# First stage of a hybrid decoder step: which engine scales the tokens and which makes their low part

## The reference, cut to what matters

```python
def rms_norm(x, g):
    xf = x.astype(jnp.float32)
    y = xf * lax.rsqrt(jnp.mean(xf * xf, axis=-1, keepdims=True) + EPS)
    return (y * g.astype(jnp.float32)).astype(x.dtype)

def hybrid_layer(x, attend, ...):
    n = rms_norm(x, g_mix)
    q, k, v, xr, gr, gates = jnp.split(n @ w_in, SPLITS, axis=-1)
    ...        # stick-breaking attention, RG-LRU branch, gates, w_out, ConvFFN, final norm
```

## Time and profile before

| | |
|---|---|
| median of 3 timed runs | 2435.93 us (2434.49 to 2438.55) |
| span of the profiled execution | 2431.0 us; the only time of that execution that is shown, 4.9 us under the median of the timed runs |
| PE busy in the span | 2178.0 us (90%) |
| DVE, ACT, POOL busy | 1433.5, 862.5, 331.6 us |
| first projection on PE starts | 51.31 us after the start of the span |

### The profile page before, as it was taken

How to read it: one execution, slowest core, us unless ns; L and a number is a source line. 1 busy time by engine, 2 the same in 40 slices (tenths; PEclk the granted TensorE clock), 3 DMA queues, 4 the chain that set the end, 5 groups by cost and what they waited for, 6 DMA issues and landing times. The chain is left out here.

```text
span 2431.0 us, 37753 instructions
## 1 busy us (share of the span) xinstructions
PE 2178.0 (90%) x12940; PEld 1926.8 (79%) x12940; DVE 1433.5 (59%) x2447; ACT 862.5 (35%) x1321; POOL 331.6 (14%) x151
## 2 busy tenths in 40 slices
PE   4997999999999999998999969789999999999986
PEld 3896777777777777777777747689999999999985
DVE  6002766767677676776768763364555554655645
ACT  4112454453544535445454452221222121222213
POOL 4122000000000000000001030031222211222210
PEclk9998998998989999999999979899999999999998
DMA  3333121031220302103021032211111111111104
GB/s 114 97 87 97 35 59 58 23 82 30 61 60 23 81 27 69 54 22 87 18 77 48 23 102 80 77 44 35 52 43 43 52 35 35 52 43 43 52 17 155
DMA packets 159829, 139.13 MB, mean 57 GB/s; under 512 B 19381, under 2 KB 147446, under 8 KB 159668
## 3 DMA queue, kind: packets, MB, share of 16 engines
q1 hardware_dynamic: 159694, 137.32, 19.1%
HBM read 119.86 MB, written 17.68 MB: 57 GB/s over the span
## 5 line engine op out<-in xcount | busy, mean ns | idle before, releaser
L87 PE MATMUL d_p_up<-n_hi,d_w_hi 128*128 128x350 f32 x1056 | 343.0, 325 | 14.0 <-POOL d_w_lo L1488 7.7
L87 PE MATMUL d_p_up<-n_hi,d_w_lo 128*128 128x350 f32 x1056 | 342.8, 325 | 0.0
L87 PE MATMUL d_p_up<-n_lo,d_w_hi 128*128 128x350 f32 x1056 | 342.5, 324 | 0.0
L1635 DVE TENSOR_TENSOR mix<-mix,d_p_down 128x350 f32<-128x350 f32 x264 | 137.3, 520 | 320.9 <-PE d_p_down L1682 320.9
L87 PE MATMUL b_p_proj<-n_hi,b_w_hi 128*128 128x350 f32 x768 | 294.8, 384 | 0.0
L1114 PE MATMUL b_p_av<-b_w_t,b_v_in 128*64 128x128 f32 (+2 forms) x1440 | 229.7, 291 | 36.1 <-DVE b_w_t L900 21.0
L87 PE MATMUL b_p_proj<-n_lo,b_w_hi 128*128 128x350 f32 x768 | 259.0, 337 | 0.0
L87 PE MATMUL b_p_proj<-n_hi,b_w_lo 128*128 128x350 f32 x768 | 258.9, 337 | 0.0
L1532 ACT ACTIVATE d_up<-d_p_up 128x350 f32<-128x350 f32 x132 | 60.8, 462 | 499.6 <-PE d_p_up L87 499.6
L797 POOL TENSOR_TENSOR b_w_lo<-w_raw,b_w_hi 128x1024 fp32r<-128x1024 f32 x33 | 84.2, 2553 | 1073.4 <-ACT b_w_hi L813 1073.4
L1114 PEld LDWEIGHTS b_p_av<-b_w_t,b_v_in 128*64 128x64 f32 (+1 forms) x1440 | 154.7, 140 | 94.1 <-issue 31.7
(11 more groups left out here) (241 smaller groups left out, 4429.5 us busy)
## 6 DMA issues: line engine op xcount, KB each, us to landing
w_raw<-in_w_in SPq DMA_DIRECT2D x45, 512.0 KB, 4.1
w_raw<-in_w_up SPq DMA_DIRECT2D x45, 512.0 KB, 3.9
b_page<-in_cache_k SPq DMA_DIRECT2D x128, 128.0 KB, 2.1
b_page<-in_cache_v SPq DMA_DIRECT2D x128, 128.0 KB, 2.0
w_raw<-in_w_down SPq DMA_DIRECT2D x22, 512.0 KB, 3.3
b_q_in<-q_scr SPq DMA_DIRECT2D x16, 264.1 KB
q_scr<-a_q_stage SPq DMA_DIRECT2D x16, 260.0 KB, 3.4
mix<-in_x_prompt SPq DMA_DIRECT2D x8, 512.0 KB, 7.0
```

The source lines that it names most:

```text
L87: last = pe.matmul(out, w[:, k, :], x[:, k, col:col + CW], start=(k == 0 and w is w_hi and x is x_hi), stop=(k == KT - 1 and w is w_lo))
L1635: dve.tensor_tensor(to, to, p_down[:, n % 4, 0:CW], ALU.add).then_inc(down_out, 1)
```

## The change

Two pieces of work move to another engine. The product of the tokens with their reciprocal root becomes an ACT activation (a copy whose scale is a column of a_stat), at the end of ACT's iteration t, behind the rounding of tile t-1 and, in iteration 7, behind the rounding of the first weight block. DVE's reciprocal raises a new semaphore, inverted, for which that activation waits. The subtraction that makes n_lo becomes a DVE instruction at the end of DVE's iteration t, for tile t-2 (in the last iteration for tiles 7 and 8). POOL keeps only the low parts of the weights.

```diff
 # GpSimd
-                for t in range(TILES):
-                    c0, nr = token_tile(t)
-                    pool.wait_ge(hi_ready, t + 1)
-                    pool.tensor_tensor(g.n_lo[:, :, c0:c0 + nr], tmp[:, t % 2, :, 0:nr],
-                                       g.n_hi[:, :, c0:c0 + nr].bitcast(F32), ALU.subtract).then_inc(lo_ready, 1)
-                    if t == TILES - 2:
-                        low_part(0, 1)
+                low_part(0, 1)
                 low_part(1, 2)
 # ScalarE, in the loop over t
                     if t in (7, 9):
                         high_part((t - 7) // 2, 3 * (t - 5) // 2, 16)
+                    if t < TILES:
+                        _, nr = token_tile(t)
+                        act.wait_ge(inverted, t + 1)
+                        act.activation(x_tok[0:nr, t, :], x_tok[0:nr, t, :], ACT.Copy,
+                                       scale=stat[0:nr, 2, t:t + 1]).then_inc(normed, 1)
 # VectorE, in the loop over t
                         dve.wait_ge(rooted, t + 1)
-                        own.step(dve.reciprocal(stat[0:nr, 2, t:t + 1], stat[0:nr, 2, t:t + 1]))
-                        dve.tensor_scalar(x_tok[0:nr, t, :], x_tok[0:nr, t, :], stat[0:nr, 2, t:t + 1], None,
-                                          ALU.mult).then_inc(normed, 1)
+                        dve.reciprocal(stat[0:nr, 2, t:t + 1], stat[0:nr, 2, t:t + 1]).then_inc(inverted, 1)
 ...
+                    for u in {TILES: (TILES - 2, TILES - 1)}.get(t, (t - 2,)):
+                        if u >= 0:
+                            c0, nr = token_tile(u)
+                            dve.wait_ge(hi_ready, u + 1)
+                            dve.tensor_tensor(g.n_lo[:, :, c0:c0 + nr], tmp[:, u % 2, :, 0:nr],
+                                              g.n_hi[:, :, c0:c0 + nr].bitcast(F32), ALU.subtract).then_inc(lo_ready, 1)
```

More of the change, by code:

```diff
@@ L126, in phase_qkv @@
         rooted = sem("a_rooted")
+        inverted = sem("a_inverted")
         normed = sem("a_normed")
```

## The result

The changed kernel takes 2442.07 us (median of 9 runs, 2437.85 to 2444.53), the kernel before, run beside it, 2436.09 us (9 runs, 2434.10 to 2438.89). The ratio is 1.0022, with a 95% interval of 1.0013 to 1.0032: slower by 5.98 us, where the prediction had 5.7. On a second chip it was 2440.03 (11 runs) against 2434.86 (23 runs), ratio 1.0020, interval 1.0012 to 1.0029, so 5.17 us. The slowdown is real; whether it is over the 0.2% that the prediction called slower can't be told from either, since both intervals hold 1.002.

What follows compares the result with a forecast made beforehand. PE, busy 90% of the span, was taken as the bound, so the first projection's start decides: +9.48 to the last tile, -3.75 behind it, +5.73 in all, added to the kernel before's median: 2441.7 us, 8 of 10 within 2437.5 to 2445.5.

Steps and rivals of the forecast that it cites:

- the 0.2%: Smallest difference from no change a measurement can tell, here 4.9 us; slower begins at 2440.8 us, given chance 0.62.
- The ring: Each tile's scaled copy, transposes, weight product and rounding follow one another, the next copy behind: 5.40 us against 5.02.
- The first tile: The copy stands behind ACT's square of tile 1, so PE's first transposes start at 8.16, 1.03 us later.
- To the last tile and behind it: Last weight product at 53.39, 9.48 us later; then DVE subtracts and the first projection starts at 57.04.
- The gain at the tail: From last weight product to first projection 3.65 us in place of 7.40, as DVE subtracts: 3.75 gained.
- The whole sum: First projection later by +9.48 up to the last weight product, less 3.75 behind it: +5.73 us.
- B: POOL's low part of the second weight block slows DVE's last subtraction to 2.48: 2442.9, or 2444.2 with tile 7's; chance 0.06.
- C: In the tiles, transposes stay hidden or run faster, so not slower: 2434.4 or 2431 us; chance 0.06.
- D: The shift is partly lost in later stages where a DMA is late: +3 remains, 2439 us; chance 0.08.
- A: PE's clock at the projections' start: up at once 2440.1 us, chance 0.12; up as much later 2443.3, chance 0.08.

Runs made afterwards that it cites:

- pure delay: The kernel before, with POOL making the first weight block's low part eight more times ahead of the last n_lo: 2454.55 us, ratio 1.0074.
- the subtraction alone: The kernel before with n_lo subtracted on DVE and the tokens still scaled on DVE: 2421.49 us, ratio 0.9936.
- the copy alone: The changed kernel with the n_lo subtraction back on POOL, the tokens still scaled on ACT: 2437.39 us, ratio 1.0006.
- copy-first kernel: The changed kernel with ACT's scaled copy of tile t put ahead of the rounding of tile t-1: 2424.80 us, ratio 0.9954.
- the weight block moved: The changed kernel with ACT's rounding of the first weight block moved behind the scaled copy of tile 7: 2439.07 us, ratio 1.0016.
- padded after: The changed kernel with 144 semaphore instructions added on PE's queue ahead of its first projection: 2428.84 us, ratio 0.9972.

## Why the prediction was right

*The ring.* Predicted 5.40, measured 5.41. The parts: copy to transposes 1.20 (11.53 to 12.71: 1.18; 16.94 to 18.12: 1.18), transposes to weight product 2.00 (2.01), weight product to rounding 1.24 (1.25), rounding to copy 0.96 (0.97). The copy's price, the one thing that no row of before showed, had been estimated from a column as scale and as bias; it is 1132 ns where 1.14 was predicted. The groups of after:

```profile
L306 ACT ACTIVATE mix<-mix,a_stat 128x1024 f32<-128x1024 f32 x8 | 9.1, 1132 | 0.0
L367 DVE TENSOR_TENSOR n_lo<-a_tmp,n_hi 128x1024 fp32r<-128x1024 f32 x8 | 9.7, 1218 | 0.0
```

The subtraction took 1218 ns against 1226 predicted. Both groups have no idle time ahead of them that another engine's wait would explain: they run as soon as their turn comes.

*The first tile.* Predicted start of the transposes 8.16, measured 8.27: the copy ended at 8.12 and the step from ACT to PE was 0.15 us and not 0.06 at this place. The weight product of tile 1 came at 14.72, predicted 14.63.

*To the last tile and behind it.* Predicted 53.39 and 57.04, measured 53.56 and 57.20. The gain at the tail, 3.75, was 3.76. The whole sum was 0.16 us short, 0.09 of it from the first tile.

*What the chip made of it.* +5.73 predicted for the first projection, +5.89 in the trace, +5.98 and +5.17 in the medians. The pure delay shows, within its interval, that such a shift passes whole. The parts alone show that the sum is not the only way to this number, but the right one: -9.9 from the subtraction alone, +7.5 from the copy alone, and +5.9 for both, not -2.4. The two don't add, since the copy alone already sets the ring of 5.41; the subtraction then gains only at the tail. The trace of before held all of that in its order of instructions.

*The rivals.* B did not come: the two last subtractions took 2.44 together, and POOL's second low part started at 56.90, 0.24 us before the last one ended. Its mechanism is real all the same: in the copy-first kernel a subtraction on DVE that meets POOL's low part (34.58, beside POOL from 33.31 to 35.68) took 2.19 us, the others 1.22. C did not come in after; its condition, a copy ahead of the rounding, was built as the copy-first kernel. It put the kernel 12 us under before, more than C's 5, since C had kept the ring's other periods. D is refuted by the pure delay. A, to which 0.20 was given, 0.08 of it to the late side, did come in the traces, on that side. PE's first projections of after, and the first piece of work on ACT behind them:

```profile
57.65 0.49 PE L87 MATMUL a_proj<-n_lo,a_w_hi 128*128 128x350 f32 x1
...
62.90 0.49 PE L87 MATMUL a_proj<-n_lo,a_w_hi 128*128 128x350 f32 x1
...
63.41 0.33 PE L87 MATMUL a_proj<-n_hi,a_w_hi 128*128 128x350 f32 x1
...
64.10 0.46 ACT L314 ACTIVATE a_kv_ch<-a_proj 128x350 f32<-128x350 f32 x1 [5.65 <-PE a_proj L87]
```

The same instruction in the kernel before:

```profile
56.96 0.47 ACT L314 ACTIVATE a_kv_ch<-a_proj 128x350 f32<-128x350 f32 x1 [8.16 <-PE a_proj L87]
```

At 0.49 us a matmul PE goes at the slower pace until 63.19, 6.0 us behind its start, against 3.4 in before. The granted clock doesn't show it: it is 1.00 in after from 57.3 to 63.0, and in before from 51.4 to 54.2. ACT's first piece comes 6.90 us behind the first projection, not 5.65, so this costs 1.25 us, close to the 1.6 of the rival; in the second profile of after it was 6.90 too. By these traces the forecast should have been 7.1 (5.89 + 1.25) and not 5.7. The medians can't tell it apart, since the granted clock, which falls to 0.50 for stretches of later stages, moves more: by the means of the two profiled executions, 0.943 and 0.946, after was at 0.50 for an estimated 278 us and before for 263, and the spans differ by 10.9 where the medians differ by 6.0. The interval of the ratio is 3.2 to 7.8 us and holds both 5.7 and 7.1, so that the forecast was met to 0.3 us is in part luck; what is shown is the shift of the first projection. Whether the slower pace lasts as long in each execution of after is open. It is no property of the ring: with the weight block moved, the same ring has ACT's first piece 5.96 us behind the first projection, and over the fourteen traces it comes 5.49 to 6.90 behind.

## What to carry to other kernels

Moving an operation to an idle engine can cost time although it takes the engine no time that is missed: in a list that is worked off in order, what counts is which wait stands ahead of it, and whether that wait closes a ring with the work of the tile before. Draw the ring start to start, with all that stands in it, and try the moved instruction one place earlier before giving up the idea. When a change has two parts, price and run each alone: here one gained 15 us and the other's place in the list took it all back.

## What the runs showed of the hardware

*Instruction fetch.* 144 additional instructions ahead of the attention stage of PE, whether transposes or semaphore increments, brought the instruction packets from 86 to 33 or 42, PE's idle time ahead of the score products for which the profile shows no wait from 25 to between 6 and 12 us, its whole idle time in the stage from 94 to 97 to between 81 and 91 us, and the stage from 1163 to 1177 to between 1144 and 1160 us. By the Trainium skill, Runtime: NRT & Kernel Launch, Instruction fetch mechanics, instructions come in blocks of 16 KiB over the engine's own queue, mostly hidden, and a taken branch to a target that isn't held forces a fetch. The trace agrees on the size of a packet (1.41 MB in 86). With 44 to 53 packets fewer, PE's idle time is 4 to 16 us of 2435 less, so not all fetches would be hidden here; the trace shows the two numbers falling together, and no wait of PE for a packet. The rest of the gain is a higher clock, for which no run shows the cause. That the branch back in the attention loop is what fetches again fits, but was only argued: the code's place was changed, not the branch. Why the kernels with ACT's copy have 42 packets and the others 33, with one and the same list on PE, is open.

*The clock.* Executions of one kernel on one chip lie up to 20 us apart, and mostly go by the granted clock: in the padded after the fastest, 2418.74 us, had 0.954, the slowest, 2439.13, 0.945; in before on that chip 0.948 and 0.943 went with 2430.74 and 2439.49. With 9 and 11 runs a difference of six us was clear of noise. The first projection in the trace was the surer measure: 57.20 and 57.24 in the two traces of after.

*A semaphore instruction* took PE 0.13 us when 72 stood in a row (9.54 us), which made the padding of 144 anything but free.

*VectorE beside GpSimd.* The token product on DVE took 0.75 to 0.88 us alone, 2.48 beside POOL's subtraction of 2.17 and 2.71 beside one of 2.40.
